# First projection chunks taken from tokens that are not yet normed, with the root multiplied in afterwards

## The reference, cut to what matters

```python
def _rmsnorm(x, w):
    y = xf * lax.rsqrt(jnp.mean(xf * xf, axis=-1, keepdims=True) + EPS)
    return y * w
z = jnp.matmul(_rmsnorm(h, mix_norm_w), w_in)      # split into rq, rk, rv, ..., 19 parts
q_a = _rope(heads(rq), positions)
k_a = _rope(heads(rk), positions) * HEAD_DIM ** -0.5
o_a = retention(q_a, k_a, heads(rv), log_gamma)    # scores * decay, then times v
```

## Time and profile before

| | us |
|---|---|
| median of the three runs | 2100.86 |
| the three runs | 2100.86, 2100.54, 2102.43 |
| time of the profiled execution | 2101.91 |
| its span (first to last instruction) | 2100.1 |
| PE busy | 2028.5 (97%) |
| DVE, ACT, POOL busy | 1230.1, 821.3, 225.5 |
| PE busy from 0 to 10, 10 to 20, 20 to 30 | 1.32, 3.38, 8.46 |
| PE busy from 30 to 80 | 49.59 |
| PE busy from 80 to 150 | 62.89 |

### The profile page before, as it was taken

One profiled execution on the slowest core, in us unless ns is written; L12 is line 12 of the kernel. 1 busy time (PEld: TensorE's weight loads), 2 busy tenths in 40 slices (PEclk: granted clock), 3 DMA queues, 4 the chain that ended last, 5 costly groups with the idle time before them and its releaser, 6 DMA issues.

```text
span 2100.1 us, 30569 instructions
## 1 busy us (share of the span) xinstructions
PE 2028.5 (97%) x13050; PEld 1782.6 (85%) x13050; DVE 1230.1 (59%) x1666; ACT 821.3 (39%) x1051; POOL 225.5 (11%) x185
## 2 busy tenths in 40 slices
PE   6988999999999999999999999999999999999998
PEld 6985898999888888888888888888888888878998
DVE  6777655767643665553555457535766744755454
ACT  6642455655532222243442222234222223455444
POOL 1000000413111001100101001110100111001111
PEclk9999999999999999999999999999999999999999
DMA  6424654454642544333124345332545533304553
GB/s 241 155 90 171 231 200 182 151 181 164 228 161 95 181 175 158 123 111 112 61 101 154 123 157 198 133 126 105 193 159 199 199 126 114 126 21 161 179 181 114
DMA packets 54136, 317.04 MB, mean 151 GB/s; under 512 B 6000, under 2 KB 12400, under 8 KB 23792
## 3 DMA queue, kind: packets, MB, share of 16 engines
q1 hardware_dynamic: 50848, 308.99, 41.3%
q10 hardware_dynamic: 3152, 6.10, 0.8%
HBM read 314.01 MB, written 1.05 MB: 150 GB/s over the span
## 4 chain that ended last, share of the span: by engine, by line
PE 84%; DVE 7%; ACT 4%; issue 3%; DMA 0%; SPq 0%; POOL 0%; DVEq 0%; ACTq 0%; POOLq 0%
PE psum L276 26%; PE psum L278 26%; PE psum L277 26%; ACT w_hi L252 2%; DVE w_lo L260 1%; PE psum L1331 1%; PE psum L1314 1%; PE psum L1733 1%; DVE work L465 1%; PE psum L1046 0%; DVE normed_lo L1916 0%; DMA raw<-in_w_in_r 0%; DVE xc L1522 0%; PE psum L1342 0%; PE psum L929 0%
## 5 line engine op out<-in xcount | busy, mean ns | idle before, releaser
L276 PE MATMUL psum<-normed_hi,w_hi 128*128 128x256 f32 (+1 forms) x2600 | 861.7, 331 | 23.9 <-DVE normed_lo L472 9.8
L277 PE MATMUL psum<-normed_lo,w_hi 128*128 128x256 f32 (+1 forms) x2600 | 851.0, 327 | 0.0
L278 PE MATMUL psum<-normed_hi,w_lo 128*128 128x256 f32 (+1 forms) x2600 | 850.4, 327 | 0.0
L260 DVE TENSOR_TENSOR w_lo<-raw,w_hi 128x2048 fp32r<-128x2048 f32 (+1 forms) x246 | 510.1, 2074 | 396.5 <-ACT w_hi L252 395.7
L276 PEld LDWEIGHTS psum<-normed_hi,w_hi 128*128 128x128 f32 x2600 | 494.2, 190 | 75.7 <-issue 25.7
L277 PEld LDWEIGHTS psum<-normed_lo,w_hi 128*128 128x128 f32 x2600 | 494.6, 190 | 43.5 <-issue 1.2
L278 PEld LDWEIGHTS psum<-normed_hi,w_lo 128*128 128x128 f32 x2600 | 494.3, 190 | 42.0
L252 ACT ACTIVATE w_hi<-raw 128x2048 fp32r<-128x2048 f32 (+1 forms) x246 | 421.6, 1714 | 162.4 <-PE psum L278 157.3
L276 PE MATMUL psum<-h_hi,w_hi 128*128 128x512 f32 (+1 forms) x913 | 311.2, 341 | 2.0 <-POOL h_lo L1678 1.7
L277 PE MATMUL psum<-h_lo,w_hi 128*128 128x512 f32 (+1 forms) x913 | 309.9, 339 | 0.0
L278 PE MATMUL psum<-h_hi,w_lo 128*128 128x512 f32 (+1 forms) x913 | 309.8, 339 | 0.0
(11 more groups left out here) (383 smaller groups left out, 1342.1 us busy)
## 6 DMA issues: line engine op xcount, KB each, us to landing
raw<-in_mod SPq DMA_DIRECT2D x72, 1024.0 KB, 4.7
raw<-in_a_up SPq DMA_DIRECT2D x42, 1024.0 KB, 4.8
raw<-in_b_up SPq DMA_DIRECT2D x42, 1024.0 KB, 4.8
raw<-in_ffn_up SPq DMA_DIRECT2D x22, 1024.0 KB, 4.9
raw<-in_a_down SPq DMA_DIRECT2D x32, 704.0 KB, 4.0
raw<-in_b_down SPq DMA_DIRECT2D x32, 704.0 KB, 4.0
raw<-in_ffn_down SPq DMA_DIRECT2D x16, 704.0 KB, 4.0
raw<-in_wo SPq DMA_DIRECT2D x8, 1024.0 KB, 4.7
```

Of the source, the lines that this page charges most:

```text
L260: dve.tensor_tensor(w_lo[:, slot, 0:size], raw[:, raw_slot(("main", g)), 0:size], w_hi[:, slot, 0:size].bitcast(F32), ALU.subtract).then_i ...
L276: pe.matmul(out, lh, rh, start=first, stop=False, skip_group_check=group)
L277: pe.matmul(out, lh, rl, start=False, stop=False, skip_group_check=group)
L278: return pe.matmul(out, ll, rh, start=False, stop=last, skip_group_check=group)
```

## The change

PE starts on chunk 0 with tokens that are multiplied with the norm's weight but not with the root ("plain" tokens). ACT and DVE make them from x directly and put them in the place `C` of the split tokens, which the memory norm needs only later. All three chunks of w_in_r take these plain tokens. The root is multiplied in afterwards: into the sines and the cosines for rq and rk, and into rv as it is copied out, which DVE now does. Chunk 0 is split in quarters. Weights are issued ahead of the small tables, and `small` (the norm's weights and other columns) is issued by ACT. The positions come with the early tables, so that the angles don't wait for the late ones. PE's list is written anew from chunk 0 to chunk 14. DVE's list changes up to the low part of chunk 6 and ACT's up to the high part of chunk 6. Behind these points the lists of DVE and ACT are as before.

```diff
+        def plain_act(act):
+            for k in range(KT):
+                act.activation(xs_hi[:, k, C], xc[:, k, X], ACT.Copy, scale=col("mix_norm_w", k)).then_inc(plain_hi, 1)
+        def plain_dve(dve):
+            for k in range(KT):
+                dve.wait_ge(plain_hi, k + 1)
+                dve.scalar_tensor_tensor(xs_lo[:, k, C], xc[:, k, X], col("mix_norm_w", k), xs_hi[:, k, C].bitcast(F32),
+                                         ALU.mult, ALU.subtract).then_inc(plain_lo, 1)
+        def first_hi(act):
+            act.wait_ge(*landed(("main", 0)))
+            for q in range(4):
...
+        def first_lo(dve):
...
 retention_dve_angles:
-            dve.wait_ge(tables_in, 16 * len(MIX))
 retention_dve_cosines:
+            sines = work[:, UP + 3 * T:UP + 4 * T]
             o(dve.tensor_tensor(kk_, sn, sn, ALU.mult))
             o(dve.tensor_scalar(kk_, kk_, -2.0, 1.0, ALU.mult, ALU.add))
+            o(dve.tensor_tensor(kk_, kk_, rstd[:, X], ALU.mult))
+            o(dve.tensor_tensor(sines, sines, rstd[:, X], ALU.mult))
 retention_dve_rotated:
+            dve.wait_ge(tables_in, 16 * len(MIX))
+        def win_evac_values(dve):
...
+            dve.tensor_tensor(z[:, RV:RV + 2, :], one_bank(s.slot, T), rstd[:, X].unsqueeze(1).to_broadcast([P, 2, T]),
+                              ALU.mult).then_inc(evacuated, 1)
 SP:
-            for name in START:
-                sp.dma_start(START[name][:], io[name]).then_inc(start_in, 16)
             for at in range(len(loads)):
                 load(sp, at)
                 if at == SLOTS - 1:
+                    for name in START:
+                        sp.dma_start(START[name][:], io[name]).then_inc(start_in, 16)
                     sp.dma_start(xc[:, :, C], io["mem"]).then_inc(mem_in, 16)
 PE:
+            win_pe_first(pe)
             pe.wait_ge(start_in, 16 * len(START))
             pe.wait_ge(set_up, 2)
             first.pe(pe)
-            win_pe(pe, "w_in_r", 0, first.ready_at_first(pe))
-            win_pe(pe, "w_in_r", 1)
-            memory.pe(pe)
-            win_pe(pe, "w_in_r", 2)
+            win_pe(pe, "w_in_r", 1, span=C)
+            win_pe(pe, "w_in_r", 2, span=C)
             retention_pe_turned(pe, ret_order)
-            win_pe(pe, "w_in_d", 0, midway=lambda: retention_pe_values(pe, ret_order), at=1)
+            win_pe(pe, "w_in_d", 0, first.ready_at_first(pe), midway=lambda: retention_pe_values(pe, ret_order), at=5)
+            win_pe(pe, "w_in_d", 1, midway=lambda: memory.pe(pe))
-            win_pe(pe, "w_in_d", 1, midway=scores)
-            win_pe(pe, "w_in_d", 2, midway=lambda: retention_pe_out(pe, ret_order))
+            win_pe(pe, "w_in_d", 2, midway=scores)
             win_pe(pe, "w_in_small", 0)
-            win_pe(pe, "w_in_b", 0)
+            win_pe(pe, "w_in_b", 0, midway=lambda: retention_pe_out(pe, ret_order))
             win_pe(pe, "w_in_b", 1)
-            win_pe(pe, "w_in_b", 2, midway=lambda: delta_pe_tok(pe, delta_order))
-            delta_pe_rows(pe, delta_order)
-            win_pe(pe, "w_in_b", 3)
-            delta_pe_sums(pe, delta_order)
-            win_pe(pe, "w_in_b", 4)
-            win_pe(pe, "w_in_g", 0)
-            win_pe(pe, "w_in_g", 1, midway=lambda: delta_pe_tokens(pe, delta_order), at=2)
+            win_pe(pe, "w_in_b", 2)
+            win_pe(pe, "w_in_b", 3, midway=lambda: delta_pe_tok(pe, delta_order))
+            win_pe(pe, "w_in_b", 4, midway=lambda: delta_pe_rows(pe, delta_order))
+            win_pe(pe, "w_in_g", 0, midway=lambda: delta_pe_sums(pe, delta_order))
+            win_pe(pe, "w_in_g", 1)
+            win_pe(pe, "w_in_g", 2, midway=lambda: delta_pe_tokens(pe, delta_order), at=2)
             delta_pe_products(pe, delta_order, ...)
-            win_pe(pe, "w_in_g", 2)
             win_pe(pe, "w_in_g", 3)
 ACT, the new list up to where it joins the old one:
+            act.dma_start(small[:, :], io["small"]).then_inc(small_in, 16)
+            plain_act(act); first_hi(act); split_hi(act, 1)
             first.act_squares(act)
+            split_hi(act, 2)
+            first.act_guess(act)
+            win_evac(act, "w_in_r", 0)
+            first.act_high(act, range(0, 4))
+            split_hi(act, 3)
+            first.act_high(act, range(4, KT))
+            win_evac(act, "w_in_r", 1)
+            retention_act(act)
+            memory.act_squares(act)
             split_hi(act, 4)
+            win_evac(act, "w_in_d", 0)
+            split_hi(act, 5)
             memory.act_guess(act)
             memory.act_high(act, range(0, 4))
             split_hi(act, 6)
             memory.act_high(act, range(4, KT))
 DVE, the same:
+            plain_dve(dve); first_lo(dve); split_lo(dve, 1)
+            retention_dve_angles(dve, ret_order)
             split_lo(dve, 2)
+            first.dve_stats(dve); the eight scalings and low parts, with split_lo(dve, 3) after the fourth
+            win_evac_values(dve)
             retention_dve_cosines(dve, ret_order)
             split_lo(dve, 4)
+            retention_dve_rotated(dve, ret_order)
+            split_lo(dve, 5)
             memory.dve_stats(dve)
             memory.dve_scaled(dve, range(0, 4))
             split_lo(dve, 6)
             retention_dve_decayed(dve, ret_order)
             memory.dve_scaled(dve, range(4, KT))
```

More of the change, by code:

```diff
@@ L261, in split_lo @@
                               ALU.subtract).then_inc(lo_ready, 1)
-        def first_splits(eng, split):
-            for g in range(2):
-                split(eng, g)
+        plain_hi, plain_lo = sem("plain_tokens_hi"), sem("plain_tokens_lo")
+        quarter_hi, quarter_lo = sem("first_quarters_hi"), sem("first_quarters_lo")
+        def plain_act(act):
[9 more added lines that the diff above has]
+            for q in range(4):
+                w = slice(q * CHUNK // 4, (q + 1) * CHUNK // 4)
+                mm = act.activation(w_hi[:, 0, w], raw[:, raw_slot(("main", 0)), w], ACT.Copy)
+                if q < 3:
+                    mm.then_inc(quarter_hi, 1)
+                else:
+                    mm.then_inc(hi_ready, 1)
+        def first_lo(dve):
+            for q in range(4):
+                w = slice(q * CHUNK // 4, (q + 1) * CHUNK // 4)
+                if q < 3:
+                    dve.wait_ge(quarter_hi, q + 1)
+                else:
+                    dve.wait_ge(hi_ready, 1)
+                mm = dve.tensor_tensor(w_lo[:, 0, w], raw[:, raw_slot(("main", 0)), w], w_hi[:, 0, w].bitcast(F32), ALU.subtract)
+                if q < 3:
+                    mm.then_inc(quarter_lo, 1)
+                else:
+                    mm.then_inc(lo_ready, 1)
         def bank_free(pe, s):
@@ L423, in act_guess @@
                 act.wait_ge(n_sum, self.j + 1)
[L424 removed]
+                act.activation(rstd[:, self.stats], psum[:, 6, 0:self.w], ACT.Abs_reciprocal_sqrt, scale=-1.0 / D, bias=col("eps")).then_inc(n_guess, 1)
                 act.wait_ge(n_guess, self.j + 1)
[L426 removed]
+                act.activation(half[:, self.stats], rstd[:, self.stats], ACT.Square, scale=(0.5 / D) ** 0.5).then_inc(n_half, 1)
             def act_high(self, act, tiles):
@@ L443, in dve_stats @@
             def dve_stats(self, dve):
-                r, t = rstd[:, 0:self.w], half[:, 0:self.w]
+                r, t = rstd[:, self.stats], half[:, self.stats]
                 dve.wait_ge(n_sum, self.j + 1)
@@ L503, in build @@
             "ret_act": dict(sines=2),
-            "ret_dve": dict(angle=6, rotated=11, v_tok=12, decayed=14, out=15),
+            "ret_dve": dict(angle=6, rotated=13, v_tok=14, decayed=16, out=17),
             "ret_pe": dict(turned=1, v_tok=2, scores=3, out=4),
@@ L1422, in build, with win_pe_first, win_pe @@
         WIN_TILES = dict(w_in_r=(RQ, RK, RV), w_in_d=(BQ, BK, BV), w_in_b=(CQ, CQ + 2, DF, CV, DI), w_in_g=(RG, BG, CG, DG))
-        def win_pe(pe, job, c, before_k=None, midway=None, at=KT // 2):
+        def win_pe_first(pe):
+            s = Step(jobs["w_in_r"], 0)
+            for n in range(2):
+                for k in range(KT):
+                    q = 2 * n + k // 4
+                    if k % 4 == 0 and q < 3:
+                        pe.wait_ge(quarter_lo, q + 1)
+                    elif k % 4 == 0:
+                        pe.wait_ge(lo_ready, 1)
+                    if n == 0:
+                        pe.wait_ge(plain_lo, k + 1)
+                    w = slice((n * KT + k) * P, (n * KT + k + 1) * P)
+                    mm = three_passes(pe, psum[:, s.slot, n * T:(n + 1) * T], (w_hi[:, s.slot, w], w_lo[:, s.slot, w]),
+                                      (xs_hi[:, k, C], xs_lo[:, k, C]), k == 0 and n == 0, k == KT - 1, group=True)
+            mm.then_inc(chunk_done, 1)
+        def win_pe(pe, job, c, before_k=None, midway=None, at=KT // 2, span=X):
             s = Step(jobs[job], c)
@@ L2292, in build @@
         first = Norm(X, lambda k, h: col("mix_norm_w", k), direct=5)
```

(26 more changed lines are left out.)

32 lines of the change are left out of this document (16 added, 16 removed).

## The result

The changed kernel takes 2111.72 us in the median of 4 runs (2110.82 to 2114.22); the kernel before takes 2100.70 in 4 runs. The ratio is 1.0049, with a 95% interval of 1.0037 to 1.0061: slower by 11.0 us. A second set of 10 runs of the same kernel, in a later series, gave 2110.60 against 2101.35 and a ratio of 1.0038 (1.0027 to 1.0048). The forecast was 2107.5 (+6.6), its range ended at 2111.5. The first set's median lies 0.2 us above the range, the second's inside it. The sign and the places are right, the size is too small.

A forecast was written before the change was run, and what follows sets the result against it. PE was taken as the bound, with time lost where it waits or a DVE and ACT chain replaces it. A 7.2 us lead, lost to two gaps and half-clock stretches, ended at +6.6: 2107.5 us, range 2102.5 to 2111.5.

The forecast's parts named there:

- The sign: Whole kernel: slower than before by more than 4.2 us, above 2105.1, given 76%.
- the places: PE waits for w_lo of 4 to 5 us at about 60 and again at 74, half clock behind both.
- The start: Chunks 0 to 3: first projection matmul at 11.7 instead of 21.5, chunk 3 done at 42.8, PE 7.2 us ahead.
- The new wait ahead of the rotated copies: Around chunk 3: PE waits 1.3 us, as chunk 1 is evacuated only at 34.7.
- The gaps: PE stands still 4.7 us before chunk 7 and 4.9 us before chunk 8.
- The output's place: Retention output moved to the middle of chunk 7, its copy ahead of chunk 8's low part: gap of 4.9 us.
- The scores: Scores moved from the middle of chunk 4 to that of chunk 5, so chunk 7 waits 4.7 us.
- The clock: Half-clock stretches behind the gaps before chunks 7 and 8 cost 2.0 us each, 4.0 together; bounds 0 and 2 x 2.8.
- the further fall, in the chain behind chunk 15: Rival: clock falls once more in the chain after 140, +2 to +4 us more, 2109.5 to 2111.5; 13%.
- my 6.6: At the first L832: 145.7 to 145.8 against 139.15, so +6.6 us, carried to the end of the kernel.
- Rigid shift behind the chain: Behind the first L832 the order is unchanged, so all of it shifts by the same +6.6 us.
- The faster one: Rival: chunk 7's and 8's low parts ready in time, PE keeps its 7.2 us lead, 2093.7; 7%.

The follow-up runs named there:

- e1_out_in_gap: Changed kernel with the retention output issued ahead of chunk 7 instead of in its middle; 2101.61 us, ratio to the kernel before 0.9996.
- e2_scores_early: Changed kernel with the retention scores issued ahead of chunk 5 instead of in its middle; 2111.37 us, ratio to the kernel before 1.0044.
- e3_low7_first: Changed kernel with chunk 7's split ahead of the memory norm's last four steps on ACT and DVE; 2103.57 us, ratio to the kernel before 1.0007.
- e4: Changed kernel with 9 more float32 matmuls that nobody reads ahead of chunk 7 and 9 ahead of chunk 8; 2106.29 us, ratio to the kernel before 1.0019.
- e5: Changed kernel with the edits of e1_out_in_gap, e2_scores_early and e3_low7_first together; 2100.61 us, ratio to the kernel before 0.9990.
- e8: Kernel before with only the three weight chunks issued ahead of the small tables and small issued by ACT; 2104.31 us, ratio to the kernel before 1.0005.
- the three edits and the fillings: e10_three_fill with 4 more matmuls before chunk 8 and 4 in the wait for token tiles; 2098.48 us, ratio to the kernel before 0.9981.
- e10_three_fill: e5 with 8 more float32 matmuls ahead of the first wait for L872, behind chunk 15; 2099.89 us, ratio to the kernel before 0.9989.
- e13_before_again: The kernel before itself run and profiled once more, unchanged; 2100.09 us in one run.

## Why the prediction was right, and where it was too small

**The start.** First matmul 10.87 (forecast 11.7); sums of the norm at 19.37 to 22.1 and at 378 ns each, so at full clock (to 22.3); evacuation of chunk 3 at 42.98 (42.8). The early start gives the 7.2 us that it was said to give (7.3): before, that evacuation stood at 50.32. The new wait ahead of the rotated copies is 1.6 (1.3).

**The gaps.** Forecast 4.7 and 4.9, measured 4.5 and 4.8; retention copy at 71.27 (about 71), chunk 8's low part at 76.54 to 78.8 (78.9). The output's place was the reason given for the second, and e1_out_in_gap shows it.

**The scores: the reason was wrong.** "The scores moved" as the cause of the first gap falls by e2_scores_early. The cause is the DVE and ACT list, in which chunk 7's split stands behind eight steps of the memory norm and behind chunk 6's split. e3_low7_first shows it. The number came out right because DVE reached the decay at 56.0, 1.0 us after the scores ended, and the path from there was summed correctly.

**The clock: the term that was mis-sized.** I took 2.0 us for each gap, 4.0 together; filling them gave back 4.4 in the profiles and 5.1 in the medians, so this part is nearly right. The forecast put the further fall, in the chain behind chunk 15, at nothing and left it to a rival with 13%. It was there in the changed kernel and in its repeat, where the chain took 11.7 and 12.1 us. The text itself gave the reasons for it: PE would wait 3 to 5 us, and 2.4 us had been enough once. The forecast had the first L872 at 145.7 to 145.8, and it came at 145.00 and 146.26: up to there the sum was right. With 2 us for the chain it would have been 2109.5.

That fall is not all an effect of the edit. Against the kernel before's first profile (10.0 us for the chain) it cost 1.7 to 2.1; against its repeat (11.4) only 0.3 to 0.7. It came in other kernels as well: 12.1 us in e2, e3 and e4, 11.1 in e1, 11.4 in e5, 11.5 in e8. Two profiles of the kernel before don't tell how often it has it.

**The baseline.** The sum ran against one profiled execution. That one had its clock low behind the token wait, which put the first L832 3.3 us later than in the repeat. By the end of the chain 1.9 of the 3.3 are left. There the changed kernel's two profiles (156.74 and 158.34) are 7.6 and 9.2 us behind the first profile of before, and 9.4 and 11.0 behind the repeat; the medians say 11.0 and 9.3. So 5.85 us at the first L872, which looked like my 6.6 confirmed, understates the change.

**Rigid shift behind the chain.** True but for the clock. Between the first profiles the difference is 7.6 us at 242 (L260 at 241.68 against 234.13) and 10.06 at the end; between the repeats it is 11.0 and 10.7. In both pairs 1.2 to 1.4 us are won at 923, where only the kernel before has the lower clock, and 1.2 to 1.3 lost at 1914, where it lasts longer in the changed kernel: the two cancel. What is left of the 2.5 us are the stretches at 1427 and 1789, 2.6 together, which the repeat of the changed kernel doesn't have. Whether those that repeat come from the edit is open; two profiles of each kernel can't show it.

The Trainium skill's page "TensorE: Matmul & The Clock Gate" (Part 1, "What's actually happening") calls the throttled state the default. The trace agrees: the changed kernel's first matmuls start 0.21 us apart from 11 to 17 us and 0.12 us apart after that, while the column says 1.00 throughout.

**Rivals.** The faster one (7.2 us kept) needed a path of under 5.6 us from the scores to chunk 7's low part; from 55.05 (L673 of 53.37 took 1.68) to 65.2 it was 10.2. With the three edits and the fillings, first L872 is 5.8 us earlier than in the kernel before, or 2.5 against its repeat: the lead could partly be kept, by changing the lists of all three engines and not PE's alone, and by filling the waits that stay.

## What to carry to other kernels

When work is moved on one engine of a kernel whose engines each follow a written list, look in the other engines' lists for what stands behind the thing that they will now wait for; here one call half a chunk too late cost more than the whole new start gained. Each new wait of the matmul engine is to be priced twice, by its length and by the slower stretch behind it, and a wait that can't be removed can be filled with matmuls that nobody reads, as long as they end before the wait does: in e10_three_fill they ran 2 us over and gave nothing. Gains of edits that are tried one by one don't add up when one wait feeds the other. Take the baseline from more than one profiled execution where the clock changes: one execution was 3.3 us off at the very point at which the two kernels were compared.

## What was not expected of the hardware

Waits of 2.2 to 2.4 us of PE were followed by the lower clock in some executions (134 us in the changed kernel, 122 before) and not in others of the same kernel (both repeats). A wait of 3.0 us in e1_out_in_gap was not followed by it, one of 2.0 in e5_all_three was. How long it then stays low differs too: behind the first gap of the changed kernel the clock was back at 1.00 in the window from 69 to 70, in the repeat it was at 0.50 from 65 to 70 throughout. Float32 matmuls with a 128 by 128 operand kept the clock up in every wait that they filled. The weights' loads moved ahead of 0.33 MB of small tables held those back until 15.05 us, where they had been there at 8.73 in e13_before_again.
